# A hybrid decoder layer on one core: LRU gate fills alternated with key and value fills

## The reference

```python
def _rglru(xb, gb, h0, conv_buf, ...):          # 512 channels
    xc = causal width-4 convolution of xb
    r  = sigmoid(block_diag(w_a) @ xc + b_a)    # gate a
    ig = sigmoid(block_diag(w_x) @ xc + b_x)    # gate x
    log_a = -8 * r * softplus(-lam)
    a = exp(log_a)
    b = sqrt(-expm1(2 * log_a)) * (ig * xc)
    h = linear recurrence h[t] = a[t] * h[t-1] + b[t]
    return h * gelu(gb)

def _mem_kv(mem, g_mem, w_k, w_v):              # 256 memory tokens
    m = rmsnorm(mem, g_mem)
    return m @ w_k, m @ w_v                     # each 256 x 1024
```

## Time and profile before

| | us |
|---|---|
| median of 3 runs | 1189.09 (1187.47 to 1190.93) |
| the profiled execution | 1190.37 |
| its span on the core | 1188.6 |
| PE busy | 1122.6 (94%) |
| DVE busy | 578.6 (49%) |
| ACT busy | 244.7 (21%) |
| POOL busy | 80.7 (7%) |
| mean granted clock of PE | 0.991 of full speed |

### The profile page before, as it was taken

One profiled execution on the slowest core, in us unless ns is written; L12 is line 12 of the kernel. 1 busy time (PEld: TensorE's weight loads), 2 busy tenths in 40 slices (PEclk: granted clock), 3 DMA queues, 4 the chain that ended last, 5 costly groups with the idle time before them and its releaser, 6 DMA issues.

```text
span 1188.6 us, 15229 instructions
## 1 busy us (share of the span) xinstructions
PE 1122.6 (94%) x6209; PEld 631.9 (53%) x6209; DVE 578.6 (49%) x1180; ACT 244.7 (21%) x523; POOL 80.7 (7%) x108
## 2 busy tenths in 40 slices
PE   5999999999999999999899899999899999999985
PEld 3566666677665444788766545555433333333322
DVE  3566599927756655743465622344531212121127
ACT  4300221255641001100033211011110111110115
POOL 4000010101000000000000000000111112111010
PEclk9999999999999999999999999999999999999998
DMA  9008550187461003200334482000679999999639
GB/s 299 28 1 183 51 47 1 49 224 255 143 264 22 1 0 128 85 1 1 125 123 146 173 318 108 36 36 36 239 274 409 412 416 418 411 411 408 254 121 386
DMA packets 65368, 209.26 MB, mean 176 GB/s; under 512 B 13561, under 2 KB 22417, under 8 KB 57073
## 3 DMA queue, kind: packets, MB, share of 16 engines
q1 hardware_dynamic: 54528, 177.68, 42.1%
q0 software_dynamic: 10640, 30.55, 7.3%
q10 hardware_dynamic: 128, 0.03, 0.0%
HBM read 187.05 MB, written 28.53 MB: 181 GB/s over the span
## 4 chain that ended last, share of the span: by engine, by line
PE 84%; DMA 8%; DVE 3%; ACT 2%; issue 1%; SPq 0%; DVEq 0%; POOLq 0%; ACTq 0%
PE bank L647 15%; PE bank L1125 11%; PE bank L826 9%; PE bank L790 8%; PE bank L891 8%; PE bank L1142 6%; DMA arena<-in_w_down 5%; PE bank L626 4%; PE bank L773 2%; PE bank L923 2%; PE bank L988 2%; PE bank L1113 2%; DMA arena<-in_w_in 1%; PE bank L1027 1%; PE bank L796 1%; PE bank L740 1%
## 5 line engine op out<-in xcount | busy, mean ns | idle before, releaser
L647 PE MATMUL bank<-arena 128*128 128x360 f32 (+1 forms) x576 | 181.9, 478 | 2.8 <-DMA arena<-in_w_in 1.8
L1125 PE MATMUL bank<-arena 128*32 128x512 f32 x1536 | 170.0, 594 | 1.0 <-DVE arena L2130 1.0
L647 PEld LDWEIGHTS bank<-arena 128*128 128x128 f32 x576 | 111.4, 195 | 70.2 <-issue 5.6
L1125 PEld LDWEIGHTS bank<-arena 128*32 128x32 f32 x1536 | 47.4, 110 | 105.2 <-issue 103.9
L826 PE MATMUL bank<-arena 128*128 128x272 f32 x448 | 103.0, 392 | 0.0
L790 PE MATMUL bank<-arena 128*128 128x512 f32 x224 | 99.2, 595 | 0.0
L891 PE MATMUL bank<-arena 128*128 128x512 f32 x224 | 97.7, 593 | 0.0
L1142 PE MATMUL bank<-arena 128*32 128x512 f32 x768 | 88.6, 602 | 6.1 <-DMA arena<-in_w_down 5.4
L826 PEld LDWEIGHTS bank<-arena 128*128 128x128 f32 x448 | 85.0, 190 | 17.4
L2134 DVE TENSOR_TENSOR arena<-arena,bank 128x256 f32<-128x256 f32 x24 | 10.1, 421 | 156.5 <-ACT arena L1405 156.5
L1227 ACT ACTIVATE arena<-bank 128x272 f32<-128x272 f32 (+5 forms) x92 | 41.0, 448 | 214.0 <-PE bank L647 133.0
(11 more groups left out here) (400 smaller groups left out, 1355.5 us busy)
## 6 DMA issues: line engine op xcount, KB each, us to landing
arena<-in_w_gate SPq DMA_DIRECT2D x32, 1024.0 KB
arena<-in_w_up SPq DMA_DIRECT2D x32, 1024.0 KB
arena<-in_w_down SPq DMA_DIRECT2D x32, 1024.0 KB, 13.7
arena<-in_ck SPq DMA_DIRECT2D x8, 1024.0 KB, 7.0
arena<-in_cv SPq DMA_DIRECT2D x8, 1024.0 KB, 5.1
arena<-work_moe SPq DMA_DIRECT2D x16, 512.0 KB, 10.6
arena<-in_w_in SPq DMA_DIRECT2D x3, 2048.0 KB, 14.9
arena<-in_x SPq DMA_DIRECT2D x8, 512.0 KB, 7.2
```

The lines of the kernel that those rows point to most:

```text
L647: last = nc.tensor.matmul(b[:, 0:w], win[slot][:, k, m * P:m * P + P], ht[:, k, c0:c0 + w], start=k == 0, stop=k == KD - 1)
L1125: last = nc.tensor.matmul(bank[2 + j % 2][t0:t0 + QT, :].rearrange("p (h n) -> p h n", h=2), xgt[j % 2][:, k, t0:t0 + QT], gu[e % GUB][:, ...
```

## The change

PE no longer makes the six gate fills of a block in a row. It makes two gate fills, the first fill of `memory(2c)`, two gate fills, the second fill of `memory(2c)`, and two gate fills; then come the key transposes and `memory(2c + 1)` as before. ACT evicts in the same new order, so both evictions of `memory(2c)` stand inside `lru_gates(c)` now, before the Tanh, where they stood behind the Exp. The number of instructions of every kind is unchanged. The key transposes of c = 1 and 2 now stand behind `memory(2c)`. The diff:

```diff
-            def memory(q):
+            def memory(q, parts=range(MT)):
 
                 pe.wait_ge(sem[f"wkv_in{q % 3}"], 16 * (q // 3 + 1))
-                for m in range(MT):
+                for m in parts:
                     b = claim(MA, ma, "ma_free")
...
-            def gates(c):
+            def gates(c, parts):
 
                 if c == 0:
                     pe.wait_ge(sem["gate_w_in"], 64)
                     pe.wait_ge(sem["xc_ok"], CT)
-                for a in range(2):
-                    for c0, w in CHUNKS:
+                for a, j in parts:
+                    for c0, w in CHUNKS[j:j + 1]:
...
             for c in range(CT):
-                gates(c)
+                gates(c, ((0, 0), (0, 1)))
+                memory(2 * c, (0,))
+                gates(c, ((0, 2), (1, 0)))
+                memory(2 * c, (1,))
+                gates(c, ((1, 1), (1, 2)))
                 if c in (1, 2):
                     key_t(c - 1)
-                memory(2 * c)
                 memory(2 * c + 1)
...
+            def drain_kv(q, parts=range(MT)):
+                for m in parts:
+                    dst = kst[q // 2][:, m, KQ * (q % 2):KQ * (q % 2) + KQ] if q < 4 else vv[:, m, KQ * (q - 4):KQ * (q - 4) + KQ]
+                    drain(MA, ma, "ma_full", dst, KQ, ACT.Copy, "ma_free")
+
             def lru_gates(c):
...
                 for a, dst in enumerate((tr, ti)):
-                    for c0, w in CHUNKS:
+                    for j, (c0, w) in enumerate(CHUNKS):
                         bias = par[:, COL[("lru_b_a", "lru_b_x")[a]] + c:][:, 0:1]
                         drain(MA, ma, "ma_full", dst[:, c0:c0 + w], w, ACT.Sigmoid, "ma_free", bias=bias)
+                        if (a, j) in ((0, 1), (1, 0)):
+                            drain_kv(2 * c, (a,))
...
             for c in range(CT):
                 lru_gates(c)
-                drain_kv(2 * c)
                 if c == 3:
```

More of the change, by code:

```diff
@@ L1313, in lru_root @@
                 nc.scalar.activation(ts_[:, :], ts_[:, :], ACT.Sqrt, scale=-1.0).then_inc(sem["sq_ok"], 1)
[L1315 to L1318, removed]
             for g in range(GRP):
```

## The result

The changed kernel takes 1214.69 us (median, 1214.13 to 1215.15) against 1189.43 of the kernel before. The ratio is 1.0221, with a 95% interval of 1.0202 to 1.0240: 25 to 26 us slower. The profiled execution took 1214.87 us, with a span of 1213.1 us and a mean granted clock of 0.978 where it was 0.991.

What follows compares the result with a forecast made beforehand. PE was taken as the bound, with 84% of the chain that ended last. Lost cover 17.0 plus clock 4.3 made 21.3 us on the profiled 1190.37: 1211.7, or 1210 for the median (chance 0.75), range 1204 to 1215.

Steps and rivals of the forecast that it cites:

- The wait after the second gate fill: PE's wait of 1.0 to 1.4 us in each block moves in front of a key fill; worth 0.
- the four other gate fills: Alternated with key fills, these may gain PE up to 0.4 us per block, if PE is what counts.
- The lost cover: Two fills can't cover the chain behind the last Sigmoid that four covered; extra 4.8, 4.3, 4.3, 3.6 us, sum 17.0.
- The granted clock: Each of four new PE waits is likely followed by a 1.2 GHz stretch; 4.3 us together, bounds 0 and 6.9.
- The table load: The Exp's load on the chain is counted at the measured 1.28 us; the skill's 2.66 would add 5.5 us together.
- Everything behind moves as a whole: All behind the loop is started by PE's progress, so it moves back and gives nothing back.
- half is given back: Rival: late expert loads don't move back with PE, so waits there go: 1205 us; chance 0.06.
- not slower: Rival: the Sqrt chain stays covered and PE wins 0.4 us a block on gate fills: 1187.5 us; chance 0.03.
- chain only, full clock: Rival: the loop's waits come, but the clock doesn't fall or falls while PE idles: 1206 us; chance 0.14.

Runs made afterwards that it cites:

- e2: The changed kernel without three of DVE's five operations between Exp and Sqrt: 1199.78 us, ratio 1.0091 to the kernel before.
- e1: The changed kernel with useless identity matmuls added behind memory(2c + 1) of each block: 1205.64 us, ratio 1.0140 to the kernel before.
- e4: The kernel before with the change made in block c = 0 alone: 1193.75 us, ratio 1.0048.
- e5: The kernel before with one fill of memory(2c) moved up behind the second gate fill: 1191.93 us, ratio 1.0035.
- e10: The kernel before with the change made in block c = 2 alone: 1196.09 us, ratio 1.0066.
- e9: The changed kernel with its two moved fills behind the first and third gate fill: 1209.92 us, ratio 1.0186 to the kernel before.
- e11: The kernel before, unchanged, run again for a second profile: 1186.80 us, ratio 0.9991.
- e8: The kernel before with one memory(2c) fill behind the first gate fill and memory(2c + 1)'s first eviction ahead of the Sqrt: 1183.95 us, ratio 0.9973.
- e12: The same kernel as e8, run again beside e11 on the same chip: 1183.88 us, ratio 0.9967 to the kernel before.
- e3: The changed kernel without one of DVE's five operations between Exp and Sqrt: 1212.08 us, ratio 1.0198 to the kernel before.
- e6: The kernel before with one fill of memory(2c) moved up behind the first gate fill: 1185.52 us, ratio 0.9988.

## Why the prediction was right in its mechanism and short in size

*The wait after the second gate fill is moved, not removed.* Right: 1.48 us stands before the first key fill in block 0 now, where 1.39 stood before the third gate fill. In block 1 nothing is left of it, and in blocks 2 and 3 only 0.89, since the gate fills before it take longer at the low clock. One reading beside it was wrong without effect: the four other gate fills gained nothing by the alternation, where I had up to 0.4 us a block (e2).

*The lost cover, 17.0 us.* Right: 17.3 in e1. By block e1 has 4.9, 4.0, 4.5 and 3.9 where 4.8, 4.3, 4.3 and 3.6 were worked out. e2, e4 and e5 moved the chain or the cover and the waits followed.

*The granted clock, 4.3 us, at most 6.9.* This is the step that failed: the low clock cost 9.8 us (8.0 in the loop, 1.8 in the GLU), more than the upper bound. That the clock would fall behind each of the four waits was right. I took the price from one place where it had been low for 3.4 us and called four times that the upper bound. But the stretches behind the four new waits were 6.8, 10.2, 10.2 and 6.8 us long, twice and three times those of the rows I had. I had argued that the wait for the Sigmoid table would hide part of the low time; it does hide some, in block 1 (it cost 1.1 us where half of the 4.3 us of low clock behind the wait would be 2.2), but in blocks 2 and 3 the table load waits for the first gate fill, so the slow fill comes before it on the chain, and the clock stayed low for 10.2 us. The long stretches go with that short idle time: e10 has both, e9 has neither. Why the clock stays low for longer there, the runs do not show. The fourth, behind which the GLU runs without a pause, cost 1.8 against the 1.72 I had.

The rule of the Trainium skill that I set beside this term, "TensorE: Matmul & The Clock Gate", section "HAM oscillation — how this bites in real kernels", that such waits make every burst start cold, is borne out: all four bursts behind the long waits of the changed loop began at 0.50.

*The table load.* By the Trainium skill's "ScalarE: Activation LUTs", section "What ACT_TABLE_LOAD costs", the Exp's load would cost 2.66 us with its drain. The chain after has 1.29 us from the load's start to the Exp's (270.78 to 272.07), as in the kernel before, and the sum was right to keep that.

*Everything behind moves as a whole.* Nearly: 27.1 us are lost up to the end of the GLU (17.3 + 9.8). The loop began 0.9 us earlier in this execution, and from the GLU's end to the end of the span it took 818.6 us instead of 820.3. In the profile of before the wait of 2.84 us in the experts had a low stretch behind it worth 1.72; the one of 2.52 us there now had none. The same kernel run again (e11) had 1.76 us there and no low stretch either, so this varies from execution to execution: these 2.6 us are luck, and leave 24.5 us of span.

In sum the forecast was 1210 in a range up to 1215, and the ratio puts the changed kernel at 1215.4 (1213.1 to 1217.6): the clock term, 5.5 us too small, carries the miss. The rivals "half is given back" and "not slower" did not happen; "chain only, full clock" (1206) is what e1 made.

## What to carry to other kernels

Evenly alternated work looks better than it is: ask for each item what long chain it lay over. Here two key fills, moved from behind to ahead of the last Sigmoid, uncovered a chain of 11 us over ACT and DVE four times, to fill waits of 1.3 us that did not even go. One fill moved to the one place where there was a wait it could cover, with an eviction taken ahead of the Sqrt, gained 3 to 4 us instead (e8, e12). And price a new PE wait with its clock: every one of 2.65 to 5.5 us in this loop was followed by a stretch at 1.2 GHz of 3.4 to 10.2 us, which can be longer than the wait itself.

## What the runs showed of the hardware that I had not expected

- The low clock did not last a fixed 3.4 us. Behind waits of 4 to 5.5 us with no short wait following, it lasted 6.8 us in seven of nine cases and 3.4 in two (after, e2, e3, e4, e9), and with a wait of 0.8 to 0.9 us following within 2.8 us of it 10.2 us (three of three, after and e10). Behind the shorter waits of e3 (3.28, 2.65 and 2.65 us), each with a second wait following, it was 3.4, 6.8 and 3.4 us. It partly began inside the wait: at 278.2 us, while PE went on at 280.68.
- Useless matmuls made the kernel faster: 66 products of the identity, in time that was idle anyway, took it from a ratio of 1.0221 to 1.0140, by keeping the clock at 1.00.
- A low stretch can follow small waits too. In e5 the clock was at 0.50 from 320.9 us for 3.4 us behind waits of 0.52 and 1.48 us, in e2 from 323.4 us behind 0.69 and 1.48, which the kernel before never showed in this loop; block 2 of both kernels has the same pair of waits and no fall. Behind single waits of 2.34 us (e6) it fell, behind 2.29 (e5) and 2.52 (after, in the experts) it did not.
